# Moving three of eighteen conditioning projections of a decoder layer into the prompt-attention head loop

## The reference, cut to what matters

```python
mod = silu(c) @ w_ada + b_ada            # (9 sequences, 1024) @ (1024, 9 * 1024)
sf1, cf1, gf1, sm, cm, gm, sf2, cf2, gf2 = split(mod, 9)
h = x + 0.5 * gf1 * swiglu(rmsnorm(x) * (1 + cf1) + sf1)          # FFN 1
u = rmsnorm(h) * (1 + cm) + sm
q_a, kv_a, k_pe, glu_in, gate_logits = split(u @ w_in)
A = latent_attention(...) @ w_attn_out    # prompt: 16 heads, causal; samples: a paged cache
B = silu(layernorm(dwconv31(glu(glu_in)))) @ w_conv_out
h = h + gm * ((sigmoid(gA) * A + sigmoid(gB) * B) @ w_out)
y = h + 0.5 * gf2 * swiglu(rmsnorm(h) * (1 + cf2) + sf2)          # FFN 2
```

## Time and profile before

| | |
|---|---|
| median of 3 runs | 1170.6 us (1170.58 to 1171.14) |
| the profiled execution's own time | 1171.14 us |
| its span | 1169.3 us |
| TensorE busy | 1136.3 us, 97% of the span |
| VectorE busy | 776.7 us, 66% |
| ScalarE busy | 584.2 us, 50% |
| GpSimdE busy | 61.9 us, 5% |
| mean granted TensorE clock | 0.987 of full |

### The profile page before, as it was taken

One profiled execution on the slowest core, in us unless ns is written; L12 is line 12 of the kernel. 1 busy time (PEld: TensorE's weight loads), 2 busy tenths in 40 slices (PEclk: granted clock), 3 DMA queues, 4 the chain that ended last, 5 costly groups with the idle time before them and its releaser, 6 DMA issues.

```text
span 1169.3 us, 26044 instructions
## 1 busy us (share of the span) xinstructions
PE 1136.3 (97%) x9613; PEld 1099.2 (94%) x9613; DVE 776.7 (66%) x1316; ACT 584.2 (50%) x1148; POOL 61.9 (5%) x128
## 2 busy tenths in 40 slices
PE   6699999999999999999999999999999999999998
PEld 3699999999898999999999999999999999999997
DVE  1655554467774788888888888888667666555542
ACT  1454443336674855555545454555566445444432
POOL 1000000010000000101010110101010000000000
PEclk8899999999999999999999999999999999999999
DMA  9588678947443251021211202031247773565551
GB/s 328 191 297 288 194 248 269 348 173 229 124 148 112 76 154 43 7 77 27 57 41 40 58 24 76 11 108 42 73 127 252 232 255 114 176 187 175 179 186 64
DMA packets 165295, 169.84 MB, mean 145 GB/s; under 512 B 25710, under 2 KB 143473, under 8 KB 165191
## 3 DMA queue, kind: packets, MB, share of 16 engines
q1 hardware_dynamic: 164695, 167.88, 45.7%
q10 hardware_dynamic: 512, 0.82, 0.2%
HBM read 167.13 MB, written 2.49 MB: 145 GB/s over the span
## 4 chain that ended last, share of the span: by engine, by line
PE 91%; DVE 2%; SPq 2%; ACT 2%; issue 1%; DMA 1%; DVEq 0%; POOL 0%; ACTq 0%
PE PS L1774 27%; PE PS L1776 26%; PE PS L1775 26%; SPq L439 2%; PE PS L1833 2%; PE PS L2148 1%; PE PS L2149 1%; PE PS L2173 1%; DMA raw<-in_w_ffn_in 1%; PE PS L1915 0%; ACT wH L681 0%; PE PS L2096 0%; PE PS L2034 0%; PE PS L2144 0%; DVE u L1153 0%
## 5 line engine op out<-in xcount | busy, mean ns | idle before, releaser
L1112 DVE TENSOR_TENSOR wL<-raw,wH 128x1024 fp32r<-128x1024 f32 (+2 forms) x208 | 245.8, 1188 | 213.4 <-ACT wH L681 211.9
L681 ACT ACTIVATE wH<-raw 128x1024 fp32r<-128x1024 f32 (+2 forms) x208 | 213.3, 1029 | 254.2 <-PE PS L1776 229.3
L1774 PE MATMUL PS<-uH,wH 128*128 128x264 f32 x1024 | 295.5, 289 | 10.0 <-DVE uL L1163 6.5
L1775 PE MATMUL PS<-uL,wH 128*128 128x264 f32 x1024 | 292.9, 286 | 0.0
L1776 PE MATMUL PS<-uH,wL 128*128 128x264 f32 x1024 | 292.4, 286 | 0.0
L1774 PE MATMUL PS<-wqH,kTH 128*128 128x336 f32 (+2 forms) x768 | 255.5, 333 | 0.0
L1776 PE MATMUL PS<-wqH,kTL 128*128 128x336 f32 (+2 forms) x768 | 246.3, 321 | 0.0
L1775 PE MATMUL PS<-wqL,kTH 128*128 128x336 f32 (+2 forms) x768 | 245.9, 320 | 0.0
L1774 PEld LDWEIGHTS PS<-uH,wH 128*128 128x128 f32 x1024 | 195.3, 191 | 12.0 <-issue 7.9
L1775 PEld LDWEIGHTS PS<-uL,wH 128*128 128x128 f32 x1024 | 195.6, 191 | 0.1
L1776 PEld LDWEIGHTS PS<-uH,wL 128*128 128x128 f32 x1024 | 194.8, 190 | 0.0
(11 more groups left out here) (322 smaller groups left out, 1513.5 us busy)
## 6 DMA issues: line engine op xcount, KB each, us to landing
raw<-in_w_ffn_in SPq DMA_DIRECT2D x88, 512.0 KB, 3.6
adaw<-in_w_ada SPq DMA_DIRECT2D x72, 512.0 KB, 6.5
raw<-in_w_ffn_out SPq DMA_DIRECT2D x32, 512.0 KB, 3.8
raw<-in_w_in SPq DMA_DIRECT2D x32, 512.0 KB, 4.7
kv<-in_cache_kv_latent SPq DMA_DIRECT2D x128, 128.0 KB, 2.0
raw<-in_w_ffn_out SPq DMA_DIRECT2D x16, 384.0 KB, 3.3
raw<-in_w_attn_out SPq DMA_DIRECT2D x8, 512.0 KB, 5.6
raw<-in_w_conv_out SPq DMA_DIRECT2D x8, 512.0 KB, 4.4
```

What stands on the lines that cost most here:

```text
L681: f(wH[:, k, 0:width], raw[:, k, 0:width], ACT.Copy).then_inc(w_hi, 1)
L1112: v.tensor_tensor(wL[:, k, 0:width], raw[:, k, 0:width], wH[:, k, 0:width].bitcast(F32), ALU.subtract).then_inc(w_lo, 1)
L1774: mm(dst, a[0], b[0], start=start, stop=False)
L1775: mm(dst, a[0], b[1], start=False, stop=False)
```

## The change

Three blocks move into the head loop. Block 13 leaves the end of FFN 1, block 14 leaves its place ahead of the loop, and block 15 leaves the end of the merge. `mod_rows(13)`, `(14)` and `(15)` now stand after `values(0)`, `values(4)` and `values(8)`, that is in iterations 1, 5 and 9, and their `mod_columns` on VectorE in iterations 3, 7 and 11; `scales(2)` moves to iteration 14. The names shift with it: `ADA_FFN` is now 13 and `ADA_ATTN` 16.

The loads of 13, 14 and 15 go to slots 0, 1 and 2 and are all issued ahead of the `state_conv` loads, the latter two after all products of the projection w_in that use `wH` and `wL`. The load of block 13 leaves FFN 1's output stage, that of block 15 and the wait in front of it leave the w_out stage.

At the end of FFN 1, `mod_rows(11)` now stands ahead of `early_squares`, and `mod_columns(11)` ahead of `invert(1)`. At the end of the merge block 16 stands ahead of `early_squares` and block 17 alone behind it. The clearing of `zbuf`'s first columns moves to GpSimdE's start, and the wait for the blocks' columns moves from `scores(1)` to the first transpose of the convolution state in iteration 14.

```diff
--- before.py
+++ after.py
@@ -56,9 +56,9 @@
 ADA_J, ADA_W = 18, 512
 
 ADA_ORDER = [2, 3, 0, 1, 4, 5, 8, 9, 6, 7, 10, 11, 12, 13, 14, 15, 16, 17]
-ADA_SLOT = [0, 1, 2, 3, 4, 5, 3, 4, 5, 3, 4, 5, 3, 6, 0, 3, 5, 6]
-ADA_FRONT, ADA_FFN, ADA_ATTN = 4, 14, 15
-ADA_BANK = [6, 2] * 5 + [6, 7, 6, 5, 1, 6, 3, 7]
+ADA_SLOT = [0, 1, 2, 3, 4, 5, 3, 4, 5, 3, 4, 5, 3, 0, 1, 2, 5, 6]
+ADA_FRONT, ADA_FFN, ADA_ATTN = 4, 13, 16
+ADA_BANK = [6, 2] * 5 + [6, 7, 6, 7, 6, 7, 3, 7]
 ADA_BETWEEN = ((6, 7), (8,), (9,))
 ADA_SLOT_FREE = {i: max(k for k in range(i) if ADA_SLOT[k] == ADA_SLOT[i]) + 1
                  for i in range(ADA_J) if ADA_SLOT[i] in ADA_SLOT[:i]}
@@ -483,7 +483,7 @@
 
             ffn_in(Q_FFN1_IN, x["w_ffn1_in"], first=True)
             ffn_out(Q_FFN1_OUT, x["w_ffn1_out"],
-                    [(i, c, min(n + c, 23)) for i, n in ((13, 1), (7, 7), (8, 10), (9, 14), (10, 16), (11, 20), (12, 23)) for c in range(4)])
+                    [(i, c, min(n + c, 23)) for i, n in ((7, 7), (8, 10), (9, 14), (10, 16), (11, 20), (12, 23)) for c in range(4)])
             win = wview(x["w_in"])
             for i in range(2):
                 for k in range(4):
@@ -540,6 +540,8 @@
             sp.wait_ge(w_lo, 4 * Q_GATE)
             ada_load(ADA_FFN)
             sp.wait_ge(w_used, 4 * Q_GATE)
+            for i in range(ADA_FFN + 1, ADA_ATTN):
+                ada_load(i)
             st = x["state_conv"].rearrange("b t n -> (b t) n")
             sp.wait_ge(use_ps, FILLED["qabs"])
             for i in range(2):
@@ -568,16 +570,13 @@
                     col = 512 * i + 256 * m
                     chunk(q + i, n % 4, v[:, 4 * half:4 * half + 4, col:col + 256], 4, 256)
                     if n in after:
-                        if after[n] == (C, (0,)):
-                            sp.wait_ge(w_used, 4 * Q_WO)
                         ada_load(*after[n])
 
-            A, B, C = ADA_ATTN + 1, ADA_ATTN + 2, ADA_ATTN
+            A, B = ADA_ATTN, ADA_ATTN + 1
             square_stage(Q_AO, wview(x["w_attn_out"].rearrange("h d n -> (h d) n")), False, {5: (A, (0,)), 7: (A, (1,))})
             square_stage(Q_CO, wview(x["w_conv_out"]), False, {1: (A, (2,)), 3: (A, (3,))})
             sp.wait_ge(w_used, 4 * Q_CO)
-            square_stage(Q_WO, wview(x["w_out"]), True,
-                         {n: (B, (n,)) if n < 4 else (C, (n - 4,)) for n in range(8)})
+            square_stage(Q_WO, wview(x["w_out"]), True, {n: (B, (n,)) for n in range(4)})
             ffn_in(Q_FFN2_IN, x["w_ffn2_in"])
             ffn_out(Q_FFN2_OUT, x["w_ffn2_out"])
             for half in range(2):
@@ -598,6 +597,7 @@
             nc.gpsimd.memset(vrow[:, :], 0.0).then_inc(memz, 1)
             nc.gpsimd.memset(ones[:, :], 1.0).then_inc(memz, 1)
             nc.gpsimd.memset(epsc[:, :], EPS).then_inc(memz, 1)
+            nc.gpsimd.memset(zbuf[:, :, 0:CW - 1], 0.0).then_inc(memz, 1)
             def early_sum(n):
 
                 for kt in range(1, SUMMED[n] + 1):
@@ -608,7 +608,6 @@
             early_sum(0)
             early_sum(1)
             pool.wait_ge(ada_used, ADA_FFN)
-            nc.gpsimd.memset(zbuf[:, :, 0:CW - 1], 0.0).then_inc(memz, 1)
             nc.gpsimd.memset(kvn[:, :], 0.0)
             nc.gpsimd.memset(ktokS[:, :, NOPE:QK], 0.0)
             nc.gpsimd.memset(lqTn[:, :, :], 0.0)
@@ -1256,11 +1255,10 @@
             own.wait()
             ffn_out(Q_FFN1_OUT, G_FFN1_OUT, GF1, False)
             mod_columns(10)
+            mod_columns(11)
             invert(1)
             prenorm(1)
-            mod_columns(11)
             mod_columns(12)
-            mod_columns(13)
 
 
             v.memset(ss6[:, :], 1.0).then_inc(ss6_set, 1)
@@ -1538,13 +1536,17 @@
                     i_ = v.tensor_copy(wq[:, :, c:c + H], qa[:, ds(b, 1), :, :].rearrange("p o k h -> p (o k) h"))
                 i_.then_inc(qx_done, 1)
 
-            mod_columns(ADA_FFN)
             mask_max(0)
             for hd in range(H):
                 if hd + 1 < H:
                     mask_max(hd + 1)
                 if hd % 4 == 1 and hd >= 5:
                     heads_out((hd - 5) // 4)
+                if hd % 4 == 3 and hd < 12:
+                    mod_columns(ADA_FFN + hd // 4)
+                if hd == 14:
+                    scales(2)
+                    own.wait()
             dve.wait_ge(rest_sb, 5)
             put_q(0, 0)
             page_lo(0, 0, 0, 0, True)
@@ -1750,12 +1752,10 @@
                     residual(4 * j + 2 * m, 4 * ((G_WO + m) % 2), KT * GM, G_WO + 2 * j + m)
                     ahead(Q_WO + j, m + 2)
                 own.end(2)
-            mod_columns(ADA_ATTN)
-            scales(2)
             invert(2)
             prenorm(2)
+            mod_columns(ADA_ATTN)
             mod_columns(ADA_ATTN + 1)
-            mod_columns(ADA_ATTN + 2)
             half_gate(GF2)
             own.wait()
             ffn_in(Q_FFN2_IN, G_FFN2_IN, FT + KT, FT)
@@ -1894,10 +1894,9 @@
                              rows=(g0 + 3, g0 + 5) if norm is None and i == n == 1 else None)
                 if norm is not None:
                     mod_rows(10)
+                    mod_rows(11)
                     early_squares(norm, 2)
-                    mod_rows(11)
                     mod_rows(12)
-                    mod_rows(13)
 
             def pairs(q0, g0, mov, lo_, hi_):
 
@@ -2082,14 +2081,11 @@
                 i_ = tr(PS[0:CW - 1 + NB, 2 + kt // 4, 128 * (kt % 4):128 * (kt % 4) + 128],
                         zbuf[:, kt, SEQ:CW - 1 + T], ident)
             i_.then_inc(use_ps, 1)
-            mod_rows(ADA_FFN)
             read(pe, "qt1")
 
 
             def scores(hd):
                 b = hd % 2
-                if hd == 1:
-                    pe.wait_ge(mod_turned, ADA_ATTN)
                 if hd >= 2:
                     pe.wait_ge(masked, hd - 1)
                 mm(PS[:, b, 0:128], qT[:, hd, 0:128], kT[:, hd, 0:128], start=True, stop=True)
@@ -2099,6 +2095,7 @@
 
                 if i == 0:
                     pe.wait_ge(in_st, 32)
+                    pe.wait_ge(mod_turned, ADA_ATTN)
                 else:
                     pe.wait_ge(st_sb, 2)
                 for kt in range(KT):
@@ -2201,6 +2198,8 @@
                 turn_probs(hd)
                 if hd >= 1:
                     values(hd - 1)
+                if hd % 4 == 1 and hd < 12:
+                    mod_rows(ADA_FFN + hd // 4)
                 if hd == 14:
                     turn_state(0)
                 if hd == 15:
@@ -2306,7 +2305,6 @@
             mod_rows(ADA_ATTN)
             early_squares(2, 2)
             mod_rows(ADA_ATTN + 1)
-            mod_rows(ADA_ATTN + 2)
             ffn_in(Q_FFN2_IN, G_FFN2_IN, 2)
             ffn_out(Q_FFN2_OUT, G_FFN2_OUT)
```

## The result

The kernel after takes 1178.72 us (median of 4 runs, 1177.85 to 1179.43), the kernel before 1170.87 us (4 runs, 1170.58 to 1172.21). The ratio is 1.006, 95% interval 1.0048 to 1.0073: slower, by 7.9 us between the medians and by 5.6 to 8.5 us by the interval. The direction was forecast, the size was not: +4.85 us was said, with 1177.4 us as the upper end.

The account below looks back on a forecast made before the run. TensorE, busy for 97% of the span, was taken to bound the kernel. The loop's 5.61 us less gains of 0.56 and 0.2 gave +4.85 us, so 1175.5 us, with a range of 1173.6 to 1177.4.

Parts of the forecast that it names:

- The end of FFN 1: Block 13 leaves, but block 11 ahead of early_squares delays the norm; the rest turns idle: gain 0.2 us.
- Ahead of the loop: Without block 14 scores(0) waits for the queries and starts at 376.95: gain 0.56 us, not 1.87.
- The loop: Three blocks added to the head loop, where TensorE sets the pace, are paid in full: 5.61 us.
- C: Rival: the head loop absorbs a good part; with half of 5.61 hidden +2.0, 1172.6 us; chance 0.06.
- D: Rival: faster; 1.87 us gained at each end, 0.56 ahead of the loop, loop free: -4.3, 1166.3 us; chance 0.07.
- The end of the merge: Only block 17 covers the norm; TensorE idles 1.87 us longer, FFN 2 starts at the same time: gain nothing.
- The loads: Twelve DMAs instead of four ahead of the state loads: cost nothing; if a page load is late, the first pages are.
- E: Rival: late state or page loads stop the first page, 2 to 5 us more, 1179 us; chance 0.03.
- The sum of the steps: Whole kernel: 5.61 - 0.56 - 0.2 + 0 = +4.85 us, own range +3.2 to +5.3.
- All 18 blocks stay, so the sum is made of idle time alone: Whole kernel: a moved block gains only TensorE's idle time at its new place and loses what it covered before.
- Rival A: One more half-clock stretch, from the three new idle gaps, costs 1.4 us: +6.25, 1176.9 us; chance 0.26.
- B: Rival: the half-clock stretch after the merge lands earlier, while TensorE waits: +3.85, 1174.5 us; chance 0.12.

Follow-up runs that it names:

- behind: The changed kernel with blocks 11 and 16 put back behind early_squares: 1175.92 us, ratio 1.0041 against the kernel before.
- before_c: The kernel before run again unchanged, for a further profile: 1168.07 us.
- before_d: The kernel before run again unchanged, for a further profile: 1172.49 us.
- dup3: The kernel before with three more, unused blocks of matmuls in the head loop (iterations 1, 5, 9): 1178.61 us, ratio 1.0064.
- Dup1: The kernel before with one more, unused block of matmuls in the head loop (head 5): 1173.23 us, ratio 1.0019.
- dup2: The kernel before with two more, unused blocks of matmuls in the head loop (heads 1 and 5): 1174.56 us, ratio 1.0027.
- dup3p: The kernel before with three unused blocks in the head loop and three eighths of one in head 7: 1178.12 us, ratio 1.0066.

## Why the prediction was wrong, and where it was right

**The end of FFN 1: gain 0.2 forecast, -0.06 measured.** The mechanism was right (block 11 ahead of early_squares delays the norm and the saved block turns into 1.32 us idle, 1.4 forecast), the small gain was not there. I gave early_squares 1.4 us by the merge's eight matmuls, but it takes 1.54 us with and without the wait, so from block 4 to early_squares it is (254.84 - 175.29) - (254.79 - 176.98) = 1.74 us more, and the norm is that much later, not 1.6. I also let w_in start with the end of the eighth; it starts 0.15 us behind it (260.56 + 0.48 = 261.04, and 261.19). The run behind shows the step directly: with block 11 back, 1.69 us are gained.

**Ahead of the loop: gain 0.56 forecast, 0.44 measured** (0.37 to 0.44 in the three profiles without a long stretch, beside the first profile of before, and 0.6 beside the mean of its five). Right, and TensorE's idle time ahead of scores(0) is 1.43 us.

**The loop: 5.61 forecast, 6.07 measured.** The mechanism was right and the size was off: I took a block's length from the chain, 1.87 us, and allowed 0.06 us for each change of work at the upper end only. The head with a block is 2.00 us longer, and two profiles with unused blocks give 2.00 and 4.02 us. Half hidden (C) and free (D) are out.

**The end of the merge: nothing forecast, nothing measured,** with 2.87 us of idle time. The order there can gain: behind got 1.08 us out of it.

**The loads** cost nothing that the chain shows; no page waited (E is out).

**The sum of the steps** was thus +4.85 forecast and +5.7 measured, 0.4 us above its own range, which had 0.2 us of room for the changeovers in the loop. What carried the time past 1177.4 is a term that the sum did not have. The step that failed is "All 18 blocks stay, so the sum is made of idle time alone": it priced every stage that the change doesn't touch at nothing. The runs show TensorE's clock in the narrow stage in its place, +3.1 us in the profiled pair and +2.1 in the mean of five and four profiles. 5.7 + 2.1 = 7.8 us, against 7.9 measured, agree more closely than these numbers can: the profiled executions themselves differ by 7.4 us in the mean, and over all executions, 6.9 us apart, only 1.2 us stand beside the 5.7. The term is thus 1 to 2 us, and its size is known no better. Rival A had the right kind of cost and the wrong place and cause. It looked for a stretch at the new idle gaps, because the one that I saw came behind idle time. In FFN 2, where A and B both looked, the first 60 products took 0, +0.06, -1.35, -1.35 and -0.03 us beside the first profile of before in its five profiles, and -0.92, -0.02, -0.75 and -0.78 in the four of after: means of -0.53 and -0.62, no difference. So the longer gap there shows neither a cost nor a gain. A and B took the stretch in FFN 2 as given, but before_c and before_d, 1.35 us shorter there, don't have it. I had the profile of before in hand with the clock at 0.50 over this window, with TensorE busy for all of it, and did not ask what moves it:

```profile
845.50:848.50 3.00, 3.00 (x15) 3.00 (x15) 0.59 (x1) 0.00 (x0) 0.00 (x0) 0.50 0.18 61
```

What TensorE had done up to then, from 841.18 us on and without a pause, was narrow matmuls. The Trainium skill (TensorE: Matmul & The Clock Gate, Part 1: The HAM clock gate) names idleness in its table of the two states as what leads to the slow one; in this stage no window has any idle time of TensorE, and the measurement decides. The same part says of the slow matmuls at a kernel's start that their number differs from run to run of one kernel, and the trace agrees for this stage too: 12.06 to 13.68 us for the same 85 matmuls of before.

Why it is worse after: the stretch begins early in the narrow work, about 2 us behind its start (the second group of 16 takes 3.60 us and 24 of the 48 gate products run slow), where in three profiles of before it began more than 4 us behind it, at the end of the narrow matmuls or just after them, and 13 to 16 gate products ran slow. In dup3's profile a loop that is longer by three blocks is enough for this, with nothing else of the change in the kernel. Shown, then: the place, what it costs in each profile, and that with most of the narrow matmuls left out it is gone from both kernels. Supported by 11 profiles against five, but not beyond chance for any one kernel: that the added time in the loop brings it. Not shown: what fixes the moment at which the clock falls. Dup1, dup2 and dup3p all had 13.7 us and none 12.1, so a rule for which added time is cheap did not come out of these runs, each with one profile, and I did not find a version that beats the kernel before.

## What to carry to other kernels

Where the chain lies on TensorE almost everywhere, moving its work can only pay if it leaves a place that another engine does not at once fill with a wait. For each place, find the instruction that starts the next sub-layer's norm and keep every block behind it: block 11 ahead of early_squares cost 1.7 us by its place alone. Price a block that goes into a tight loop by the lengthening of the iteration and not by its busy time, and where the granted clock falls in a busy stage, allow 1 to 3 us (1.6 and 3.1 here) for any change of the time ahead of it; look at the granted clock of every busy stage, and take several profiles before a cause is named.

## What the hardware did that I had not expected

- The clock falls while TensorE is busy. Within or right behind the 36 recorded matmuls with snew and olrow (4.76 us without a pause before) it went to 0.50 for 3.4, 6.8 or 10.2 us in each of nine profiles of the two kernels, and with 28 of them left out it stayed at 1.00. Narrowness alone isn't it: the 64 recorded matmuls of 8 columns of w_uv that follow take 2.06 us at full clock. Window over them in the first profile of before:

```profile
853.26:857.50 4.24, 4.24 (x82) 4.15 (x82) 2.73 (x6) 3.66 (x9) 0.00 (x0) 1.00 0.61 144
```

- Matmuls of 16 columns suffer from it as much as wide ones: 16 recorded ones took 1.96 us at full clock and 3.60 at half, a product 0.12 and 0.22.
- A block of 64 matmuls between the parts of two heads costs 0.14 us beside its own 1.86.
- The same stage of the same kernel took 12.06 or 13.68 us from one execution to the next, and the stage ahead of the loop differed by 2.6 us. One profile of each kernel would have put the excess at 3.1 us; five and four put it at 2.1, and the times of all executions at 1.2.
